# Up product of three of four feed-forward blocks as seven quarter products, with the conditioning pieces dealt out anew

## The chip, the cores and the metric

The kernel runs on one core of one Trainium2 chip. The metric is device time in microseconds (us) of one launch. TensorE (PE) does the matrix products, VectorE (DVE) and ScalarE (ACT) the elementwise work, GpSimd (POOL) small powers and some transfers, and SyncE's queue (SP) issues most of the weight loads. In the trace a weight load into TensorE is a row of PEld. Every float32 matrix instruction of 128 rows shows there as two entries, so that 32 instructions of the program are 64 entries of the trace.

## The reference

Two layers; in each, a feed-forward block, a token mixer, and a second feed-forward block. Touched are the feed-forward blocks and the conditioning:

```python
def swiglu(h, w13, w2):
    g, u = jnp.split(h @ w13, 2, axis=-1)
    return (jax.nn.silu(g) * u) @ w2
...
    for l in range(DEPTH):
        mod = (c_act @ ada_w[l] + ada_b[l]).reshape(bsz, N_SUB, 3, D_MODEL)
        h = modulated_norm(x, norm_w[l, 0], mod[:, 0])
        x = x + 0.5 * mod[:, 0, 2, None] * rmsnorm(swiglu(h, ffn_w13[l, 0], ffn_w2[l, 0]), norm_w[l, 1])
        h = modulated_norm(x, norm_w[l, 2], mod[:, 1])
...
        h = modulated_norm(x, norm_w[l, 4], mod[:, 2])
        x = x + 0.5 * mod[:, 2, 2, None] * rmsnorm(swiglu(h, ffn_w13[l, 1], ffn_w2[l, 1]), norm_w[l, 5])
```

There are 256 tokens, a width of 1024, an inner width of 2816; all is float32.

## The kernel before

A feed-forward block is named (l, f): layer l, first (f = 0) or second (f = 1) of the layer. It has an up phase and a down phase.

**Up phase.** The inner width is cut into FJ = 11 tiles j of 256 columns of gate and 256 columns of up. The weights of a tile (2 MB, two transfers) lie in one of two slots of `ring`. The normed input lies turned in `hT` (8 blocks of 128 channels, 256 tokens). Tile 0 is multiplied token half by token half as `hT` becomes ready (`open_by_token`, 64 products of 128 columns). The ten others go through `up(j)`: four outputs of 128 x 256, each a sum over 8 channel blocks, so 32 products of 256 moving columns. ScalarE takes the sigmoid of the gate half (its line 2037), VectorE makes sigmoid times gate times up in two operations into `actA` (line 2376). TensorE's tile j waits for the activation of tile j - 2, whose PSUM banks it takes over, and SP loads tile j + 2 when the product of tile j is done (line 735).

**Conditioning.** The modulation rows of later stages are vector-matrix products with 1024 x 1024 blocks of `ada_w`. Each row is streamed in four pieces of 1 MB (`PIECES`, three buffers, line 700), and VectorE multiplies and adds the two 128 x 1024 halves of a piece (`conditioning_pieces`, lines 2379 and 2382). When the four are done, TensorE sums over the partitions (`conditioning` in `beside`) and VectorE adds the bias. `COND_PLAN` says which rows belong to which block, `UP_PIECES` how many pieces follow each tile. All of them stood in the up phases.

**Down phase.** The product with `w2` is already made by seven quarter products of 512 moving columns (`down_1` to `down_7`), over six loads of weights (`DOWN_PAIRS`); VectorE makes sums of activations and of weights for each (`down_sums`, t and w). The last three keep two of the seven for the end (`HELD`). Then `after_down` forms the rows, the norm and the next stage's input.

The order of each engine is the order in which its code is written; there is no scheduler. VectorE's order in the up phase is the loop of `ffn` in its block: two operations of activation, evacuation of finished rows, pieces.

## Time and profile before

| | us |
|---|---|
| median of 3 runs | 2684.61 |
| lowest, highest | 2684.23, 2687.25 |
| the profiled execution | 2689.09 |
| span of its core in the profile | 2687.3 |
| TensorE busy | 2579.1 |
| VectorE busy | 1576.9 |

One execution is profiled. The span runs from its first to its last instruction; 1.8 us of the launch lie around it. A group row of the profile gives the number of entries, their busy time (overlapping ones counted once) and the mean duration of one. For pipelined matrix products the mean is longer than the distance from one to the next, so the pace of TensorE is read from the start of a run of equal entries and the start of the next run.

### The profile page before, as it was taken

What the parts mean: (1) busy time and instruction counts of PE and PEld (TensorE: products, weight loads), DVE (VectorE), ACT (ScalarE), POOL (GpSimd) and SP (SyncE); (2) the same over time, 40 slices, a digit from 0 to 9 for tenths busy, and PEclk for the clock granted to TensorE, in tenths of its full rate; (3) what the DMA queues carried; (4) which work ended last, traced back from release to release, by engine and by line L of the source; (5) the groups of instructions that cost most, each with busy time, mean ns of one, the idle gap of its engine ahead of it and who ended that gap; (6) DMA issues with size and microseconds to landing.
All of it is one profiled execution on the core that took longest, in us unless ns stands there. A gap on an engine that the chain in (4) does not pass through costs nothing.

```text
span 2687.3 us, 66122 instructions
## 1 busy us (share of the span) xinstructions
PE 2579.1 (96%) x29733; PEld 1889.3 (70%) x29733; DVE 1576.9 (59%) x2765; ACT 500.7 (19%) x1017; POOL 233.1 (9%) x372
## 2 busy tenths in 40 slices
PE   7999999999998999999999999999999999999998
PEld 6884877787775555588578758778778745556883
DVE  3566455677775866445644355556787758563225
ACT  1000232122221332100010011322222123321000
POOL 6000102000101101010000010110010011010000
PEclk9999999999899999999999999999999999999999
DMA  9885433222326543399576444423222275335443
GB/s 357 315 286 180 134 128 111 93 97 80 109 90 211 181 164 109 134 352 328 199 243 235 141 161 145 155 85 106 95 88 93 86 248 195 135 115 203 157 157 125
DMA packets 238987, 445.10 MB, mean 166 GB/s; under 512 B 8920, under 2 KB 103702, under 8 KB 238704
## 3 DMA queue, kind: packets, MB, share of 16 engines
...
## 4 chain that ended last, share of the span: by engine, by line
PE 82%; DVE 9%; DMA 3%; issue 3%; ACT 2%; SPq 1%; POOL 1%; DVEq 0%; POOLq 0%; ACTq 0%
PE ps L1152 80%; DVE scratch L2376 5%; DMA ring<-in_ffn_w 2%; DVE scratch L2379 1%; DVE scratch L2382 1%; DMA scratch<-acs_scratch 1%; DVE gbc L2382 1%; DMA ring<-in_w_in 1%; PE ps L1181 1%; DVE scratch L2728 1%; DMA acs_scratch<-scratch 0%; DVE x L2382 0%; PE ps L1834 0%; ACT scratch L2201 0%; ACT scratch L2199 0%
## 5 line engine op out<-in xcount | busy, mean ns | idle before, releaser
L1152 PE MATMUL ps<-hT,ring 64*64 64x256 f32 (+2 forms) x9216 | 1144.8, 373 | 9.9 <-issue 3.4
L1152 PEld LDWEIGHTS ps<-hT,ring 64*64 64x64 f32 (+1 forms) x9216 | 935.9, 159 | 147.6 <-issue 18.5
L1152 PE MATMUL ps<-scratch 64*64 64x32 f32 (+5 forms) x14824 | 661.7, 246 | 56.4 <-DVE scratch L2376 25.7
L1152 PEld LDWEIGHTS ps<-scratch 64*64 64x64 f32 (+2 forms) x14824 | 516.2, 140 | 240.9 <-issue 116.6
L1152 PE MATMUL ps<-ring,hT 64*64 64x256 f32 (+2 forms) x2816 | 425.4, 423 | 4.6 <-DVE scratch L2382 2.6
L2376 DVE TENSOR_TENSOR scratch<-scratch,ps 128x512 f32<-128x512 f32 (+2 forms) x324 | 163.0, 503 | 411.9 <-ACT scratch L2037 342.0
L1152 PE MATMUL ps<-ring,scratch 128*128 128x512 f32 x864 | 393.2, 594 | 2.8 <-DVE scratch L2379 1.3
L2376 DVE TENSOR_TENSOR scratch<-scratch 128x256 f32<-128x256 f32 (+4 forms) x522 | 314.7, 603 | 86.3 <-ACTq L2184 30.5
L1152 PEld LDWEIGHTS ps<-ring,hT 64*64 64x64 f32 (+1 forms) x2816 | 229.3, 151 | 141.2 <-issue 115.0
L1152 PEld LDWEIGHTS ps<-ring,scratch 128*128 128x128 f32 x864 | 158.8, 190 | 173.8 <-issue 165.9
L2382 DVE SCALAR_TENSOR_TENSOR scratch<-scratch,ccol 128x1024 f32<-128x1024 f32 x120 | 154.3, 1286 | 8.3 <-DMA scratch<-in_ada_w 4.1
L2037 ACT ACTIVATE scratch<-ps 128x512 f32<-128x512 f32 x44 | 26.3, 597 | 579.2 <-PE ps L1152 579.2
L2376 DVE TENSOR_TENSOR scratch<-ps,lvl 128x128 f32<-128x128 f32 (+1 forms) x224 | 73.8, 329 | 70.8 <-PE ps L1152 68.1
L2382 DVE SCALAR_TENSOR_TENSOR scratch<-ps,der,scratch 128x255 f32<-128x255 f32 (+1 forms) x112 | 54.0, 482 | 92.7 <-ACTq L2064 89.2
L2379 DVE TENSOR_SCALAR scratch<-scratch 128x64 f32<-128x64 f32 (+6 forms) x256 | 85.3, 333 | 38.1 <-ACTq L2350 14.4
L949 POOL TENSOR_TENSOR stat<-stat,mhalf 128x1 f32<-128x1 f32 x24 | 14.6, 609 | 931.8 <-DVE stat L2379 931.7
L2134 ACT ACTIVATE scratch<-ps 128x512 f32<-128x512 f32 x48 | 26.5, 595 | 256.8 <-PE ps L1152 256.8
L2376 DVE TENSOR_TENSOR scratch<-ring 128x1024 f32<-128x1024 f32 (+1 forms) x24 | 27.3, 1136 | 57.2 <-DMA ring<-in_ffn_w 57.0
L2062 ACT ACTIVATE scratch<-ps,der 128x256 f32<-128x256 f32 (+1 forms) x56 | 26.5, 473 | 146.6 <-PE ps L1152 145.3
L1042 POOL TENSOR_TENSOR scratch<-scratch 128x1024 f32<-128x1024 f32 x8 | 19.8, 2474 | 298.9 <-ACT scratch L2101 298.9
L2376 DVE TENSOR_TENSOR scratch<-ps,rmask 128x512 f32<-128x512 f32 x64 | 44.2, 691 | 2.2
L1027 POOL TENSOR_TENSOR scratch<-scratch,mhalf 128x4 f32<-128x4 f32 x16 | 16.6, 1037 | 309.5 <-DVE scratch L2379 309.5
...
## 6 DMA issues: line engine op xcount, KB each, us to landing
...
ring<-in_ffn_w SPq DMA_DIRECT2D x88, 1024.0 KB, 7.7
scratch<-in_ada_w SPq DMA_DIRECT2D x66, 1024.0 KB, 7.3
...
```

Source lines behind the costliest of these rows:

```text
L949: pool.tensor_tensor(stat[:, to + t:to + t + 1], stat[:, mean + t:mean + t + 1], mhalf[:, 0:1], ALU.pow).then_inc(rstd_ready.sem, 1)
L1027: pool.tensor_tensor(gstat[:, 3, :], gstat[:, 2, :], mhalf[:, 0:CH], ALU.pow).then_inc(gn_rstd.sem, 1)
L1042: pool.tensor_tensor(v, v, zsig, ALU.mult).then_inc(silu_product.sem, 1)
L1152: return pe.matmul(o, lhsT, rhs, start=start, stop=stop)
L1181: ins = pe.transpose(ps[:, 4 + 2 * t + kt // 4, (kt % 4) * P:(kt % 4 + 1) * P], of[:, t, kt * P:(kt + 1) * P], ident[:, :])
L2037: act.activation(sgm[:, j % 2, :], ps[:, 2 * ((j + 1) % 2), :], ACT.Sigmoid).then_inc(ffn_sig.sem, 1)
L2062: own.step(act.activation(dst, ps[0:cols, 2 * pair + m // 2, (m % 2) * S:(m % 2 + 1) * S], ACT.Identity, scale=der[0:cols, ds(mcol, 1)]))
L2134: act.activation(dst, ps[:, FILL_BANKS[r], :], ACT.Identity).then_inc(fill_evac.sem, 1)
L2376: return dve.tensor_tensor(o, i0, i1, op)
L2379: return dve.tensor_scalar(o, i0, s1, s2, op0, op1)
L2382: return dve.scalar_tensor_tensor(out=o, in0=i0, scalar=s, in1=i1, op0=op0, op1=op1)
L2728: own.step(dve.tensor_tensor_scan(gi.rearrange(f512), reset[:, :, :].rearrange("p a b -> p (a b)"), lwb.rearrange(f512), 0.0, ALU.mult, AL ...
```

## The change

In blocks (0, 1), (1, 0) and (1, 1) the tiles 1 to 10 go through `up_seven(j)`. The product is seen as 2 x 2 blocks: the channels in two halves, the columns as gate and up, the tokens in two halves. Seven products of quarters (m1 to m7, each 2 x 4 instructions of 128 moving columns) take the place of eight. Block (0, 0) and every tile 0 stay as they were.

VectorE makes four sums of the input once a block (`token_sums`) and four sums of weights per tile (`up_sums`), and puts the seven results together (`opening_sums`, `closing_sums`). The input's sums lie where the down phase keeps its own (`tsum`), the weights' sums where it keeps its sums of weights (`esets`), each tile in the set that the other parity's down sums use. ScalarE copies m1 out of PSUM (`first_up`) and takes the sigmoid of the finished sums of the tile before. In VectorE's order of iteration j stand: closing and gating of tile j - 1, the pieces, the opening of tile j, the weight sums of tile j + 1. The product m6 of tile j + 1 waits for those sums, m4 for ScalarE's copy and the input's sums. A ring slot is free after m7, with two of the seven products to go.

The pieces are 24, 24, 12 and 4 in the four blocks before, and 24, 16, 20 and 4 now, of which four each in (0, 1) and (1, 0) now follow the weight sums of the down phase. The last row of these two blocks is summed over the partitions in the down phase, before its last weights. In the first part of the down phase `down_5(0)` is behind `down_7(0)`.

```diff
 COND_PLAN = {(0, 0): tuple((0, k) for k in range(2, 8)),
-             (0, 1): ((0, 8),) + tuple((1, k) for k in range(5)),
-             (1, 0): tuple((1, k) for k in range(5, 8)),
+             (0, 1): ((0, 8), (1, 0), (1, 1), (1, 3)),
+             (1, 0): tuple((1, k) for k in (2, 4, 5, 6, 7)),
              (1, 1): ((1, 8),)}
 COND_ORDER = ((0, 0), (0, 1)) + tuple(itertools.chain(*(COND_PLAN[l, f] for l in range(DEPTH) for f in range(2))))
-UP_PIECES = (2, 2, 2, 3, 2, 3, 2, 3, 2, 3, 0)
+UP_PIECES = {(0, 0): (2, 2, 2, 3, 2, 3, 2, 3, 2, 3, 0),
+             (0, 1): (0, 1, 2, 1, 2, 1, 2, 1, 2, 0, 0),
+             (1, 0): (1, 2, 1, 2, 1, 2, 1, 2, 2, 2, 0),
+             (1, 1): (1, 1, 1, 1, 0, 0, 0, 0, 0, 0, 0)}
+DOWN_PIECES = {(0, 0): (0, 0, 0, 0, 0, 0), (0, 1): (0, 1, 2, 0, 1, 0), (1, 0): (0, 1, 2, 0, 1, 0), (1, 1): (0, 0, 0, 0, 0, 0)}
+SEVEN = {(0, 0): (), (0, 1): tuple(range(1, FJ)), (1, 0): tuple(range(1, FJ)), (1, 1): tuple(range(1, FJ))}
+SEVEN_ORDER = ("m1", "m2", "m4", "m6", "m7", "m5", "m3")
...
-                    pieces_next(UP_PIECES[j - 2])
+                    pieces_next(UP_PIECES[l, f][j - 2])
                 for i in range(DOWNS):
                     down_weights(i)
+                    pieces_next(UP_PIECES[l, f][FJ - 2 + i] if i < 2 else DOWN_PIECES[l, f][i - 2])
...
+                def up_seven(j):
+                    up_ready(j)
+                    par = ffn_item(f, j) % 2
+                    w = ring[:, par, :].rearrange("p (k u n) -> p k u n", k=KT, u=2)
+                    pair, third, sets = 2 * ((j + 1) % 2), 6 + j % 2, kset[j % 2]
+                    t0, t1, half = slice(0, P), slice(P, 2 * P), KT // 2
+                    def quarter(bank, side, weights, tokens):
+                        for m in range(2):
+                            at = 256 * side + m * P
+                            for k in range(half):
+                                ins = mm(ps[:, bank, at:at + P], weights(k, slice(m * P, m * P + P)), tokens(k), k == 0, k == half - 1)
+                        ins.then_inc(up_done.sem, 1)
+                    quarter(third, 0, lambda k, c: w[:, k, 0, c], lambda k: hT[:, k, t0])
+                    quarter(pair, 0, lambda k, c: w[:, half + k, 0, c], lambda k: hT[:, half + k, t0])
+                    pe.wait_ge(*copied(l, f, f"s1_{j}"))
+                    pe.wait_ge(*made(l, f, "turned"))
+                    quarter(third, 0, lambda k, c: w[:, half + k, 1, c], lambda k: turned_4[:, k, :])
+                    pe.wait_ge(*made(l, f, f"w_{j}"))
+                    quarter(pair, 1, lambda k, c: sets[1][:, k, c], lambda k: turned_2[:, k, :])
+                    quarter(pair + 1, 0, lambda k, c: w[:, k, 1, c], lambda k: turned_3[:, k, :])
+                    quarter(pair + 1, 1, lambda k, c: sets[0][:, k, c], lambda k: turned_1[:, k, :])
+                    quarter(third, 1, lambda k, c: sets[2][:, k, c], lambda k: hT[:, half + k, t1])
...
-                    up(j)
+                    if seven((l, f), j):
+                        up_seven(j)
+                    else:
+                        up(j)
...
-                early = [c for c in COND_PLAN[l, f] if c not in late_sums(l, f)]
+                early = [c for c in COND_PLAN[l, f] if c not in late_sums(l, f) + list(last_sums(l, f))]
                 pe.wait_ge(*cond_evac(0, cond_count(*early[-1])))
                 if f and l + 1 < DEPTH:
                     pe.wait_ge(*params_evac(l + 1, 1))
...
                 down_2(0)
                 pe.wait_ge(*down_sum(l, down_sum_count(f, "t0")))
                 sums_ready(0)
-                down_5(0)
+                pe.wait_ge(*made(l, f, f"act_{FJ - 2}"))
                 down_3(0)
-                pe.wait_ge(*act_ready(l, f * FJ + FJ - 1))
                 down_6(0)
                 down_7(0).then_inc(down_step.sem, 1)
-                pe.wait_ge(*act_ready(l, f * FJ + FJ))
+                pe.wait_ge(*made(l, f, f"act_{FJ - 1}"))
+                down_5(0)
                 down_4(0).then_inc(down_step.sem, 1)
                 for c in late_sums(l, f):
                     conditioning(*c, bank=2)
...
+                    if i == HELD[1]:
+                        for c in last_sums(l, f):
+                            conditioning(*c, bank=2)
...
+                def sigmoid_of_sums(j):
+                    act.wait_ge(*made(l, f, f"g_{j}"))
+                    act.activation(sgm[:, j % 2, :].rearrange("p (t n) -> p t n", t=TT), sums[:, j % 2, 0:4:3, :],
+                                   ACT.Sigmoid).then_inc(up_copied.sem, 1)
                 for j in range(FJ):
-                    if j >= 2:
-                        act.wait_ge(*act_ready(l, f * FJ + j - 1))
-                    act.wait_ge(*up_done(l, f * FJ + j + 1))
-                    act.activation(sgm[:, j % 2, :], ps[:, 2 * ((j + 1) % 2), :], ACT.Sigmoid).then_inc(ffn_sig.sem, 1)
+                    if seven((l, f), j):
+                        act.wait_ge(*product(l, f, f"m1_{j}"))
+                        act.activation(first_up[:, j % 2, :], ps[:, 6 + j % 2, 0:256], ACT.Identity).then_inc(up_copied.sem, 1)
+                        if seven((l, f), j - 1):
+                            sigmoid_of_sums(j - 1)
+                    else:
+                        if seven((l, f), j - 1):
+                            sigmoid_of_sums(j - 1)
+                        if j >= 2:
+                            act.wait_ge(*made(l, f, f"act_{j - 2}"))
+                        act.wait_ge(*product(l, f, f"up_{j}"))
+                        act.activation(sgm[:, j % 2, :], ps[:, 2 * ((j + 1) % 2), :], ACT.Sigmoid).then_inc(up_copied.sem, 1)
+                if seven((l, f), FJ - 1):
+                    sigmoid_of_sums(FJ - 1)
...
+                if i < 2 and seven((l, f), FJ - 1):
+                    dve.wait_ge(*product(l, f, f"m7_{FJ - 1}"))
...
+            def token_sums(l, f):
+                dve.wait_ge(*hT_act(l, hT_count(3 if f else 1, 1, KT // 2 - 1)))
+                b11, b12, b21, b22 = (hT[:, KT // 2 * i:KT // 2 * i + KT // 2, t * P:t * P + P] for i in range(2) for t in range(TT))
+                own.step(tt(turned_3, b22, b12, ALU.subtract))
+                own.step(tt(turned_1, b12, b11, ALU.subtract))
+                own.step(tt(turned_2, b22, turned_1, ALU.subtract))
+                raised(tt(turned_4, b21, turned_2, ALU.subtract), made(l, f, "turned"))
+            def up_sums(l, f, j):
+                item = ffn_item(f, j)
+                par = item % 2
+                w = ring[:, par, :].rearrange("p (k u n) -> p k u n", k=KT, u=2)
+                a11, a12, a21, a22 = (w[:, KT // 2 * i:KT // 2 * i + KT // 2, u, :] for u in range(2) for i in range(2))
+                s1, s2, s4 = kset[j % 2]
+                dve.wait_ge(*slot_loaded[par](l, loads_before(item, par) + 2))
+                own.step(tt(s1, a21, a22, ALU.add))
+                own.step(tt(a21, a11, a21, ALU.subtract))
+                own.step(tt(s2, s1, a11, ALU.subtract))
+                raised(tt(s4, a12, s2, ALU.subtract), made(l, f, f"w_{j}"))
             def ffn(l, f):
                 asked = conditioning_pieces(l, f)
+                def pieces_next(n):
+                    for _ in range(n):
+                        next(asked, None)
+                def side_by_side(bank):
+                    return ps[:, bank, :].rearrange("p (a n) -> p a n", a=2)
+                def opening_sums(j):
+                    dve.wait_ge(*copied(l, f, f"s1_{j}"))
+                    dve.wait_ge(*product(l, f, f"m6_{j}"))
+                    m1 = first_up[:, j % 2:j % 2 + 1, :].to_broadcast([P, 2, 256])
+                    own.step(tt(sums[:, j % 2, 0:4:2, :], m1, side_by_side(2 * ((j + 1) % 2)), ALU.add))
+                def closing_sums(j):
+                    pair, s = 2 * ((j + 1) % 2), sums[:, j % 2]
+                    dve.wait_ge(*product(l, f, f"m5_{j}"))
+                    own.step(tt(s[:, 1:4:2, :], s[:, 2:3, :].to_broadcast([P, 2, 256]), side_by_side(pair + 1), ALU.add))
+                    own.step(tt(s[:, 2, :], s[:, 1, :], ps[:, pair + 1, 256:512], ALU.add))
+                    dve.wait_ge(*product(l, f, f"m3_{j}"))
+                    raised(tt(s[:, 1:4:2, :], s[:, 1:4:2, :], side_by_side(6 + j % 2), ALU.add), made(l, f, f"g_{j}"))
+                def gated(j):
+                    by, s = sgm[:, j % 2, :].rearrange("p (t n) -> p t n", t=TT), sums[:, j % 2]
+                    dve.wait_ge(*copied(l, f, f"sig_{j}"))
+                    own.step(tt(by, by, s[:, 0:4:3, :], ALU.mult))
+                    for t in range(TT):
+                        ins = tt(actA[:, j, :, t * P:t * P + P], by[:, t, :].rearrange("p (m n) -> p m n", m=2),
+                                 s[:, 1 + t, :].rearrange("p (m n) -> p m n", m=2), ALU.mult)
+                        if t == 0:
+                            own.step(ins)
+                    raised(ins, made(l, f, f"act_{j}"))
+                    conditioned(j)
...
+                if SEVEN[l, f]:
+                    token_sums(l, f)
                 for j in range(FJ):
                     parity, bank = j % 2, 2 * ((j + 1) % 2)
+                    if seven((l, f), j - 1):
+                        closing_sums(j - 1)
+                        gated(j - 1)
+                    if seven((l, f), j):
+                        pieces_next(UP_PIECES[l, f][j])
+                        opening_sums(j)
+                    if seven((l, f), j + 1):
+                        up_sums(l, f, j + 1)
                     if j == FJ - 1:
                         down_sums(l, f, 0)
-                    dve.wait_ge(*ffn_sig(l, f * (FJ + 1) + j + 1))
-                    own.step(tt(sgm[:, parity, :], sgm[:, parity, :], ps[:, bank, :], ALU.mult))
-                    raised(tt(actA[:, j, :, :], sgm[:, parity, :], ps[:, bank + 1, :], ALU.mult), act_ready(l, f * FJ + j + 1))
-                    if f and l + 1 < DEPTH and j == 2:
-                        read_params(l + 1, 6)
-                        derive_params()
-                    for c in summed_in(l, f, j - 1) if j < FJ - 1 else ():
-                        conditioning(*c)
-                        if c == (l, 8):
-                            dve.wait_ge(*late_weights_loaded(l, 1))
-                            gate_weights(2, merged[:, 0, :])
-                        if c == (l + 1, 1):
-                            scale_weights(0)
-                    for _ in range(UP_PIECES[j]):
-                        next(asked, None)
+                    if not seven((l, f), j):
+                        dve.wait_ge(*copied(l, f, f"sig_{j}"))
+                        own.step(tt(sgm[:, parity, :], sgm[:, parity, :], ps[:, bank, :], ALU.mult))
+                        raised(tt(actA[:, j, :, :], sgm[:, parity, :], ps[:, bank + 1, :], ALU.mult), made(l, f, f"act_{j}"))
+                        conditioned(j)
+                        pieces_next(UP_PIECES[l, f][j])
+                if seven((l, f), FJ - 1):
+                    closing_sums(FJ - 1)
+                    gated(FJ - 1)
                 down_sums(l, f, 1)
                 for c in late_sums(l, f):
-                    conditioning(*c, bank=2)
+                    evacuate_conditioning(c, 2)
...
-                    scale_weights(1)
-                    scale_weights(2)
                     for i in range(2):
                         gate_weights(i, nbc[:, i, :])
+                pieces_next(DOWN_PIECES[l, f][1])
                 for i in range(2, DOWNS):
                     down_sums(l, f, i)
+                    pieces_next(DOWN_PIECES[l, f][i])
+                for c in last_sums(l, f):
+                    evacuate_conditioning(c, 2)
                 own.restart()
```

TensorE, the start of the up phase of block (0, 1): tile 0, then tiles 1 to 4 (`hT` input, `ring` weights, `scratch` sums, `prow` parameters, `ones` the sums over partitions). Before:

```order
L1152 MATMUL ps<-hT,ring 128x128 x36
L1152 MATMUL ps<-hT,ring 128x256 x64
L1212 MATMUL ps<-ident,prow 128x128 x4
L1152 MATMUL ps<-scratch,ones 128x512 x2
L1152 MATMUL ps<-hT,ring 128x256 x64
```

Now:

```order
L1230 MATMUL ps<-hT,ring 128x128 x52
L1230 MATMUL ps<-scratch,ring 128x128 x8
L1230 MATMUL ps<-scratch 128x128 x8
L1230 MATMUL ps<-scratch,ring 128x128 x8
L1230 MATMUL ps<-scratch 128x128 x8
L1230 MATMUL ps<-hT,scratch 128x128 x8
L1230 MATMUL ps<-hT,ring 128x128 x16
L1230 MATMUL ps<-scratch,ring 128x128 x8
```

Tile 1 is 56 instructions of 128 columns (the last 16 of the first row and the five rows of 8) where it was 32 of 256; m1 and m2 read what is loaded, the other five also sums that VectorE made.

VectorE in block (0, 1). Before, tiles 0 to 2: an activation in two operations, then the pieces:

```order
L2376 TENSOR_TENSOR scratch<-scratch,ps 128x512 x2
L2379 TENSOR_SCALAR scratch<-scratch,ccol 128x1024
L2382 SCALAR_TENSOR_TENSOR scratch<-scratch,ccol 128x1024 x3
L2376 TENSOR_TENSOR scratch<-scratch,ps 128x512 x2
L2382 SCALAR_TENSOR_TENSOR scratch<-scratch,ccol 128x1024 x4
L2376 TENSOR_TENSOR scratch<-scratch,ps 128x512 x2
```

Now, iteration 2: closing and gating of tile 1, two pieces, the opening of tile 2, the weight sums of tile 3:

```order
L2505 TENSOR_TENSOR scratch<-scratch,ps 128x2x256
L2505 TENSOR_TENSOR scratch<-scratch,ps 128x256
L2505 TENSOR_TENSOR scratch<-scratch,ps 128x2x256
L2505 TENSOR_TENSOR scratch<-scratch 128x512
L2505 TENSOR_TENSOR scratch<-scratch 128x2x128 x2
L2511 SCALAR_TENSOR_TENSOR scratch<-scratch,ccol 128x1024 x4
L2505 TENSOR_TENSOR scratch<-scratch,ps 128x2x256
L2505 TENSOR_TENSOR scratch<-ring 128x1024
L2505 TENSOR_TENSOR ring<-ring 128x4x256
L2505 TENSOR_TENSOR scratch<-scratch,ring 128x1024
L2505 TENSOR_TENSOR scratch<-ring,scratch 128x1024
```

Per tile VectorE has eleven operations besides the pieces, where it had two.

TensorE in the down phase of block (0, 1), from the first held weights to the last row's sum. Before:

```order
L1152 MATMUL ps<-ring,scratch 128x512 x8
L1152 MATMUL ps<-scratch 128x512 x2
L1152 MATMUL ps<-ring,scratch 128x512 x6
L1152 MATMUL ps<-scratch 128x512 x2
L1152 MATMUL ps<-ring,scratch 128x512 x4
```

Now:

```order
L1230 MATMUL ps<-ring,scratch 128x512 x8
L1230 MATMUL ps<-scratch 128x512 x2
L1230 MATMUL ps<-ring,scratch 128x512 x2
L1230 MATMUL ps<-ones,scratch 32x1 x32
L1230 MATMUL ps<-ring,scratch 128x512 x4
L1230 MATMUL ps<-scratch 128x512 x2
```

The sum of the last row stands between the second held weights and the last.

## Rows read from the trace of the kernel before

**Rows 1.** The page: busy time by engine, and the chain that ended last.
```profile
PE 2579.1 (96%) x29733; PEld 1889.3 (70%) x29733; DVE 1576.9 (59%) x2765; ACT 500.7 (19%) x1017; POOL 233.1 (9%) x372
PE 82%; DVE 9%; DMA 3%; issue 3%; ACT 2%; SPq 1%; POOL 1%; DVEq 0%; POOLq 0%; ACTq 0%
```

**Rows 2.** Stretches, tile 1 to the down phase: (0, 1), (1, 0), (1, 1). Header first.
```profile
core 0: us, PE busy (x) PEld busy (x) DVE busy (x) ACT busy (x) POOL busy (x), PEclk, DMA share, GB/s
1151.70:1296.30 144.60, 144.60 (x847) 125.36 (x847) 81.87 (x86) 5.97 (x10) 1.56 (x3) 1.00 0.89 317
1382.40:1524.00 141.60, 141.60 (x775) 123.68 (x775) 51.13 (x55) 5.97 (x10) 0.00 (x0) 1.00 0.63 216
2472.20:2612.10 139.90, 139.90 (x647) 122.55 (x647) 32.60 (x38) 5.97 (x10) 0.00 (x0) 1.00 0.49 161
```

**Rows 3.** Timeline of TensorE in block (0, 1): start, length, engine, line, entries.
```profile
1135.97 6.43 PE L1152 MATMUL ps<-hT,ring 128*128 128x128 f32 x56
...
1143.72 35.83 PE L1152 MATMUL ps<-hT,ring 128*128 128x128 f32 x200
...
1181.54 27.79 PE L1152 MATMUL ps<-hT,ring 128*128 128x256 f32 x128
1209.26 0.71 PE L1152 MATMUL ps<-ones,scratch 128*32 128x1 f32 x64
1209.90 27.89 PE L1152 MATMUL ps<-hT,ring 128*128 128x256 f32 x128
...
1252.29 1.88 PE L1152 MATMUL ps<-scratch,ones 128*128 128x512 f32 x4
1254.00 27.79 PE L1152 MATMUL ps<-hT,ring 128*128 128x256 f32 x128
```

**Rows 4.** First tile 0 of the program, TensorE by form; then its stretch's clock.
```profile
L1152 PE MATMUL ps<-hT,ring 128*128 128x128 f32 x128 | 17.0, 303 | 2.7 <-DMA ring<-in_ffn_w 2.7
...
34.60:52.00 17.40, 17.30 (x131) 17.25 (x132) 2.33 (x8) 1.58 (x5) 15.75 (x26) 0.85 1.04 395
```

**Rows 5.** VectorE by form, whole span: count, busy us, mean ns, idle before.
```profile
L2382 DVE SCALAR_TENSOR_TENSOR scratch<-scratch,ccol 128x1024 f32<-128x1024 f32 x120 | 154.3, 1286 | 8.3 <-DMA scratch<-in_ada_w 4.1
L2376 DVE TENSOR_TENSOR scratch<-scratch 128x512 f32<-128x512 f32 x188 | 134.1, 714 | 36.7 <-ACTq L2184 30.5
L2376 DVE TENSOR_TENSOR scratch<-scratch,ps 128x512 f32<-128x512 f32 x132 | 90.7, 687 | 359.7 <-ACT scratch L2037 342.0 <-PE ps L1152 15.0
L2376 DVE TENSOR_TENSOR scratch<-scratch 128x256 f32<-128x256 f32 x208 | 88.4, 425 | 23.9 <-PE ps L1152 14.3 <-POOL scratch L1027 2.4
L2376 DVE TENSOR_TENSOR scratch<-ring 128x1024 f32<-128x1024 f32 x20 | 24.5, 1225 | 51.8 <-DMA ring<-in_ffn_w 51.7
L2376 DVE TENSOR_TENSOR gbc<-gbc,ps 128x1024 f32<-128x1024 f32 x6 | 7.3, 1220 | 0.2
```

**Rows 6.** ScalarE by form, whole span: a copy out of PSUM, an activation in SBUF.
```profile
L2234 ACT ACTIVATE scratch<-ps 128x256 f32<-128x256 f32 x32 | 12.2, 382 | 109.3 <-PE ps L1152 109.3
L2212 ACT ACTIVATE scratch<-scratch 128x512 f32<-128x512 f32 x16 | 10.1, 630 | 64.0 <-DVE scratch L2376 64.0
```

**Rows 7.** Timeline of ScalarE and VectorE after tile 0 of block (0, 1).
```profile
1151.96 0.60 ACT L2037 ACTIVATE scratch<-ps 128x512 f32<-128x512 f32 x1 [5.23 <-PE ps L1152]
1152.59 1.41 DVE L2376 TENSOR_TENSOR scratch<-scratch,ps 128x512 f32<-128x512 f32 x2 [6.84 <-ACT scratch L2037]
1154.03 0.75 DVE L2379 TENSOR_SCALAR scratch<-scratch,ccol 128x1024 f32<-128x1024 f32 x1
```

**Rows 8.** The page: one of the transfers of a tile's weights, issue to landing.
```profile
ring<-in_ffn_w SPq DMA_DIRECT2D x88, 1024.0 KB, 7.7
```

**Rows 9.** The chain in order of time at the end of block (0, 1)'s down phase.
```profile
1337.38 6.57 DMA ring<-in_ffn_w
1344.04 1.24 DVE scratch L2376
...
1347.82 1.24 DVE scratch L2376
1349.19 13.97 PE ps L1152 x32
```

85 lines of the change are left out of this document (72 added, 13 removed).

## The prediction

> **What bounds the kernel now.** First the page's busy times and the chain that ended last: TensorE is busy for 96% of the span and makes up 82% of the chain, VectorE is busy for 59% [rows 1]. Then the three stretches that the change rewrites, from tile 1 to the down phase: TensorE is busy in every one of their 144.6, 141.6 and 139.9 us, and VectorE for 81.9, 51.1 and 32.6 us of them [rows 2]. So each microsecond taken from TensorE there is won, as long as VectorE and ScalarE keep pace, and VectorE has 63, 90 and 107 us to give. Third the timeline of TensorE: two tiles of 32 instructions start at 1181.54 and the next work at 1209.26, so a tile is 13.86 us and an entry of 256 columns 216.6 ns [rows 3].
>
> **TensorE's term.** A tile becomes 7 x 16 = 112 entries of 128 columns. The trace has such entries in tile 0: 56 in 6.43 us, of which the last 0.275 is its own drain, so 112 ns from one to the next; and in the run of 200 from 1143.72 the first 72 take 35.45 less 127 x 0.2166, or 7.94 us, 110 ns each [rows 3]. These runs have a wait every fourth instruction, so waits already met cost nothing visible. I take 111 ns: a quarter product is 1.78 us, a tile 12.43, a saving of 1.43 a tile and of 43 us for 30 tiles. That is the ceiling.
>
> The Trainium skill, "TensorE: Matmul & The Clock Gate", section "Back-to-back issue gap", speaks against products of so few columns: with a weight load each, 128 columns go at about 81 ns in bfloat16 where a lone product needs 56. By that ratio, an estimate from the page, an entry would be near 155 ns and a tile 17.4 us, 106 us lost in 30 tiles. The trace disagrees: half of 216.6 is 108.3, and 110 to 112 were measured with a fresh load before each [rows 3].
>
> **VectorE's term.** Per iteration it now has: closing 0.69 + 0.42 + 0.69; the sigmoid's way out and back 0.63 + 2 x 0.03, in which it waits; gating 0.71 + 2 x 0.425; opening 0.69; four weight sums of 1.225; with 0.03 between operations (1152.59 to 1154.03 for two of 0.69) [rows 5, 6, 7]. Sum: 1.89 + 0.69 + 1.65 + 0.72 + 5.02 = 9.97 us. A piece is two of 1.286, so 2.63, and 0.53 less for the first of a row, whose first half takes 0.75 [rows 5, 7]. A gate row's evacuation is 1.25, its scaling 1.3 [rows 5]. Against 12.43 us of TensorE: no piece fits with room, one makes 12.6, two make 15.2.
>
> The wait that decides is m6 of tile j + 1, 5.33 us into its tile, on the weight sums at the end of iteration j. Behind it stand m7, m5, m3 of the tile and all later tiles. I follow both engines with T the start of tile 1.
>
> Block (1, 1): iterations 4 to 10 have no piece. VectorE waits for m6 of its tile (T_j + 7.3), opens, makes the sums and is done 13.0 after T_j, 4.8 before they are wanted. The four single pieces end at 14.2 at worst, also in time. The up stretch is 10 x 12.43 + 1.72 for the gate row's sum (1254.00 less 1252.29) [rows 3] = 126.0, against 139.9. The down phase's first weight sums wait for m7 of tile 10, then take 6.8 us: ready 0.2 us late. **-13.6 us.**
>
> Block (0, 1): tile 2's weights are asked for at T, as the slot was tile 0's. I give them 8.5 us, the median 7.7 and the issue of two [rows 8]; so the sums of tile 2 are done at T + 13.5. Iterations 2 to 8: 7 x 9.97 = 69.8, eleven pieces less two firsts 27.9, parameter copy and rows 4.3: the sums of tile 9 are done at T + 115.5. TensorE alone would want them at 8 x 12.43 + 5.33 + 2.8 for transposes and rows = 107.5. So some 8 us of waits gather by tile 9, in pieces of 2 to 3; after it no tile has a piece and nothing is late. End: 115.7 + 7.1 + 12.43 + 0.7 = T + 135.9, first down wait 0.2, against 144.6. **-8.5 us.**
>
> Block (1, 0): its pieces begin in iterations 0 and 1 (1 and 2), so the sums of tile 2 end at T + 16.5. Iterations 2 to 9: 79.8, thirteen pieces less three firsts 32.6, rows 2.7: T + 131.6, where TensorE alone would want them at 9 x 12.43 + 5.33 + 4.1 = 121.3. Waits of 10.5 us, the largest about 4 before tile 10, whose two predecessors have two pieces each. End T + 138.9; the down phase's first sums come at 143.5 and are wanted at 142.3: + 1.2. Together 140.1 against 141.6; two small rows more in the down phase (0.64 each, 1209.90 less 1209.26 [rows 3]), one of which fills the wait before the last weights. **-0.6 us.** Here the whole gain of TensorE is given back.
>
> **Parts priced at nothing.** ScalarE's copy of m1 (0.38 [rows 6]) ends 2.4 us into a tile, m4 wants it at 3.6; cover 1.2. The input's four sums (2.9 us) and tile 1's weight sums (5.0) begin once `hT` is whole, some 2 us after 1143.72 [rows 3], and end 3 us before m6 of tile 1 wants them. The slot is freed two products before the end instead of at it, and the load has 11.6 us until VectorE wants it. SP's pieces wait for VectorE's sums, and are asked for three ahead; the weights queued behind them wait for a later m7 anyway. Eight pieces in two down phases, 21 us on VectorE: it enters the phase some 6 us later than before, and by my count is level by the second held weights. The phase ends in a chain over the last load: 6.6 us of transfer, 4.9 us of sums, then TensorE [rows 9]. VectorE must have its pieces behind it when that load lands; in (0, 1) by about 2 us, in (1, 0) by about 1. If not, each phase costs up to 2.6, one piece; bounds 0 and +5.
>
> Sum: -13.6 - 8.5 - 0.6 = -22.7; I take **-22**. The profiled span of 2687.3 becomes 2665, and the median, 2684.6, becomes **2662.6**; the profiled execution (2689.09) lay 4.5 above the median, and the difference is taken over.
>
> **Bounds of the unknown.** Entry: 110 to 133 ns, the latter from the first tile 0, 17.0 us for 128, but at a granted clock of 0.85 [rows 4]; I take 111, since all the stretches show 1.00 [rows 2]. Operations in 2 x 256 views of PSUM and on a broadcast stand in no row; nearest are 0.687 and 0.714 for plain 512 [rows 5]. Each 0.1 us more per iteration costs 0.9 in (0, 1) and 0.8 in (1, 0). Between -0.3 and +0.8 per iteration that is -5 to +14. Landing up to 12 us: +2. Each wait may bring a stretch at a lower clock: the first tile 0 lost 17.0 - 14.2 = 2.8 us so; for the two waits over 3 us at most +5.
>
> **The rivals.**
> 1. VectorE keeps up everywhere. For it: it is busy for only 59% now. Against: its iteration is a chain with two rounds to other engines. It needs 9.97 to shrink to near 9, as with a shorter sigmoid's way. Then 2684.6 - 41 = 2644.
> 2. Only (1, 1) gains. For it: eleven operations a tile behind semaphores, down phases with little room. At + 0.5 us per iteration and + 4 in the down phases: 2684.6 - 22 + 8.5 + 4 = 2675.
> 3. Slower: VectorE's iteration is the pace of (0, 1) and (1, 0), and above 11.3 us it gives back more than (1, 1) wins: 22 / 17 = 1.3 us more. At + 2 us, as if each of the three PSUM views and the split gating took half as long again and the engines' rounds 0.3 more, it is 2684.6 - 22 + 34 = 2697. Against: no row of VectorE shows a view that costs so much; the copies and sums of 512 all lie at 0.69 to 0.71 [rows 5].
> 4. The 128-column products pay for their weights after all: from 124 ns an entry, 13.86 a tile, nothing is won; at 133, +1.0 a tile, 2715. Against it stand the 184 entries of rows 3.
>
> **How the numbers follow.** Forecast (-14 to -32) 0.65; rival 1 (beyond -32) 0.07; rival 2 (-5.4 to -14) 0.13; no change within 5.4 us 0.08; rivals 3 and 4 0.07. 0.2% of the time, 5.4 us, is about what a measurement of this kernel tells from no change: faster 0.85, same 0.08, slower 0.07. The range takes the forecast with its bounds and rival 2: 2651 to 2679.
>
> **What would show it.** In the profile after: entries of 128 columns 110 to 112 ns apart; stretches of 136, 139 and 126 us; TensorE waiting for VectorE's weight sums (the operations `scratch<-ring,scratch`) 8 and 11 us in the first two and not at all in the third; waits at tiles 6, 7 and 9, and at 6, 8 and 10. VectorE idle before gating about 0.7 us a tile where it is late and 2 where it is not. The end of each down phase with a wait of at most 1.5 us. It would be wrong if an iteration without pieces is over 10.5 us, if tiles of (1, 1) are over 12.6, or if TensorE waits in the held part of a down phase.

## The result, and the profile after

The changed kernel takes 2671.59 us (median of four runs, 2668.59 to 2673.89) where the kernel before took 2684.65 beside it (four runs, 2684.23 to 2687.25). The ratio is 0.9949, with a 95% interval of 0.9931 to 0.9966: faster, by 13.1 us or half a per cent. Timed again, with five runs beside nine of before, it was 2670.49 against 2686.51, ratio 0.9941 (0.9924 to 0.9959), or 16.0 us. The forecast was 2662.6, a gain of 22, so 60 to 73% of the expected gain came, with a time inside the range.

The page of the profile after: busy times, and the shares of the chain that ended last.

```profile
PE 2544.8 (95%) x31173; PEld 1901.2 (71%) x31173; DVE 1812.4 (68%) x3047; ACT 513.3 (19%) x1047; POOL 235.2 (9%) x372
...
PE 72%; DVE 18%; DMA 4%; issue 3%; ACT 2%; SPq 1%; POOL 1%; DVEq 0%; POOLq 0%; ACTq 0%
```

Against [rows 1], TensorE has 34 us less to do, and the span fell by 21 (2687.3 to 2666.6). In the chain TensorE lost ten points, to VectorE above all: for part of the time VectorE now sets the pace. The three stretches of [rows 2], from tile 1 to the down phase, show where. Columns: the window and its length, busy time of PE, PEld, DVE, ACT and POOL, the granted clock, the DMA share and GB/s.

```profile
1145.90:1284.80 138.90, 131.80 (x1258) 129.62 (x1257) 121.11 (x144) 10.11 (x20) 1.52 (x3) 0.99 0.77 267
1371.00:1514.50 143.50, 135.05 (x1194) 132.05 (x1193) 129.42 (x146) 10.11 (x20) 0.00 (x0) 0.96 0.77 269
2464.80:2591.50 126.70, 126.70 (x1126) 125.74 (x1125) 99.67 (x120) 10.00 (x20) 0.00 (x0) 1.00 0.56 183
```

In (1, 1) TensorE is busy throughout and the stretch fell from 139.9 to 126.7. In (0, 1) it fell from 144.6 to 138.9, with 7.1 us of idle TensorE; in (1, 0) it grew from 141.6 to 143.5, with 8.4 us of idle TensorE and a granted clock of 0.96. VectorE is busy for 121 and 129 us there.

The timeline of TensorE in the up part of (1, 0), around tiles 6 and 10 (start, length, what; in brackets the idle time before and who ended it):

```profile
1444.43 2.81 PE L1230 MATMUL ps<-scratch 128*128 128x128 f32 x16 [2.19 <-DVE scratch L2505]
1447.03 2.86 PE L1230 MATMUL ps<-scratch,ring 128*128 128x128 f32 x16
...
1498.61 1.95 PE L1230 MATMUL ps<-scratch,ring 128*128 128x128 f32 x16
1504.54 3.78 PE L1230 MATMUL ps<-scratch 128*128 128x128 f32 x16 [3.98 <-DVE scratch L2505]
1508.11 3.03 PE L1230 MATMUL ps<-scratch,ring 128*128 128x128 f32 x16
1510.98 1.95 PE L1230 MATMUL ps<-scratch 128*128 128x128 f32 x16
1512.77 1.95 PE L1230 MATMUL ps<-hT,scratch 128*128 128x128 f32 x16
```

A quarter product at full clock is the last pair of rows: 1.79 us from one to the next, 111.7 ns an entry. Ahead of m6 TensorE waits for the weight sums, and in these two places the two quarters behind the wait take 6.4 us (1504.54 to 1510.98) and 5.3 (1444.43 to 1449.73) instead of 3.6. Such quarters are called slow below. The granted clock in the windows around the slow quarters of tiles 7 of (0, 1), 6 and 10 of (1, 0):

```profile
1233.50:1241.20 7.70, 5.50 (x35) 5.35 (x34) 6.69 (x9) 0.63 (x1) 0.00 (x0) 0.78 0.52 204
1442.00:1449.80 7.80, 5.61 (x36) 5.42 (x35) 6.79 (x9) 0.63 (x1) 0.00 (x0) 0.78 0.52 204
1500.40:1511.00 10.60, 6.62 (x35) 6.47 (x34) 8.00 (x11) 0.63 (x1) 0.00 (x0) 0.68 0.38 151
```

Cut into slices of 1 us, the trace has the granted clock at 0.50, the 1.2 GHz level, in part of each of them: from about 1237 to 1241, 1445.4 to 1449 and 1504.5 to 1510, behind waits of 2.19, 2.19 and 3.98 us.

To compare kernels I cut each trace at the start of the second part of tile 0 (the run that starts at 1143.72 in [rows 3]) and at the first down product. Up part and down part of each block, and the two mixers, whose code none of these kernels touches, in us:

| | (0, 1) | (1, 0) | (1, 1) | three blocks | two mixers |
|---|---|---|---|---|---|
| before | 152.6 + 78.1 | 149.6 + 77.3 | 147.9 + 75.2 | 680.7 | 1732.7 |
| before, again | 152.6 + 78.8 | 149.6 + 77.2 | 147.9 + 74.3 | 680.4 | 1727.0 |
| after | 147.0 + 78.2 | 151.6 + 79.0 | 134.8 + 75.1 | 665.6 | 1727.6 |
| after, again | 147.0 + 78.7 | 150.4 + 78.8 | 134.8 + 74.9 | 664.6 | 1726.3 |
| e1: (1, 1) only | 150.0 + 78.2 | 150.5 + 77.8 | 134.8 + 74.4 | 665.6 | 1736.7 |
| e2: not (1, 0) | 148.6 + 77.7 | 150.5 + 77.9 | 134.8 + 74.5 | 663.9 | 1729.2 |
| e3: half pieces | 137.0 + 77.4 | 137.4 + 78.2 | 134.8 + 75.0 | 639.8 | 1726.4 |
| e4: three whole tiles | 140.4 + 77.5 | 141.1 + 78.2 | 134.8 + 74.7 | 646.7 | 1726.3 |
| e4 again | 140.0 + 77.6 | 141.1 + 78.1 | 134.8 + 74.6 | 646.2 | 1729.5 |
| e5: m4 again | 146.9 + 77.4 | 148.8 + 79.8 | 134.8 + 75.1 | 662.8 | 1735.2 |
| e6: even deal, two whole | 137.8 + 78.9 | 138.7 + 82.4 | 134.8 + 74.5 | 647.2 | 1733.8 |
| e7: even deal | 139.1 + 83.1 | 146.5 + 83.4 | 134.8 + 75.3 | 662.2 | 1730.0 |
| e8: e6 and e4 joined | 137.8 + 80.1 | 140.7 + 79.5 | 134.8 + 75.1 | 648.0 | 1732.7 |

The mixers differ by up to 10 us between the profiles, and by 5.7 in two of the kernel before. So the 20.7 us between the first two profiled spans are not the change alone: the blocks, which repeat within about 1 us in two profiles of before, of after and of e4, give 680.5 less 665.1, or 15.4 us, between the two timed differences of 13.1 and 16.0. The mixers' length goes with the clock that they were granted: cut into eleven slices each, the second mixer has 1.00 in all of them in the second profile of after (861.5 us) and 0.96 to 0.98 in four in e1's (868.4), and the first mixer has 0.91 in one and 0.98 in three in the first profile of before (869.7) against 0.96 in one in the second (864.6), with the same code. From here on blocks are compared.

### The profile page after: what moved, and what is told of

It reads as the page before. It is cut to its first block, busy times and chain, and to the rows that moved or that the text cites. A ratio compares the mean times of both kernels' runs of the same rounds, so it can differ in the third digit from the quotient of the medians.

```text
span 2666.6 us, 69449 instructions
## 1 busy us (share of the span) xinstructions
PE 2544.8 (95%) x31173; PEld 1901.2 (71%) x31173; DVE 1812.4 (68%) x3047; ACT 513.3 (19%) x1047; POOL 235.2 (9%) x372
## 4 chain that ended last, share of the span: by engine, by line
PE 72%; DVE 18%; DMA 4%; issue 3%; ACT 2%; SPq 1%; POOL 1%; DVEq 0%; POOLq 0%; ACTq 0%
PE ps L1230 71%; DVE scratch L2505 10%; DVE scratch L2511 3%; DMA ring<-in_ffn_w 2%; DVE scratch L2508 1%; DVE ring L2505 1%; DVE gbc L2511 1%; DVE scratch L2943 1%; DMA ring<-in_w_in 1%; PE ps L1259 1%; DMA scratch<-acs_scratch 0%; DVE x L2511 0%; DMA acs_scratch<-scratch 0%; ACT scratch L2149 0%; ACT scratch L2330 0%
## 5 line engine op out<-in xcount | busy, mean ns | idle before, releaser
L1230 PE MATMUL ps<-hT,ring 64*64 64x256 f32 (+2 forms) x8256 | 839.3, 359 | 10.7 <-issue 4.6
L1230 PE MATMUL ps<-scratch 64*64 64x32 f32 (+8 forms) x15768 | 772.9, 246 | 70.4 <-DVE scratch L2505 37.0
L1230 PEld LDWEIGHTS ps<-scratch 64*64 64x64 f32 (+3 forms) x15768 | 622.9, 142 | 255.4 <-issue 116.4
L1230 PEld LDWEIGHTS ps<-hT,ring 64*64 64x64 f32 (+1 forms) x8256 | 680.8, 156 | 99.1 <-issue 19.5
L2505 DVE TENSOR_TENSOR scratch<-scratch 128x256 f32<-128x256 f32 (+5 forms) x612 | 361.1, 590 | 104.5 <-ACTq L2313 30.4
L1230 PEld LDWEIGHTS ps<-ring,hT 64*64 64x64 f32 (+1 forms) x2816 | 227.9, 150 | 139.9 <-issue 113.0
L2505 DVE TENSOR_TENSOR scratch<-scratch,ps 128x512 f32<-128x512 f32 (+2 forms) x384 | 196.3, 511 | 165.7 <-PE ps L1230 79.5
L1230 PE MATMUL ps<-scratch,ring 128*128 128x128 f32 x960 | 120.2, 280 | 0.0
L1230 PEld LDWEIGHTS ps<-scratch,ring 128*128 128x128 f32 x960 | 115.6, 197 | 0.0
L2505 DVE TENSOR_TENSOR scratch<-ring,scratch 128x1024 f32<-128x1024 f32 (+1 forms) x54 | 64.0, 1186 | 1.9
L2505 DVE TENSOR_TENSOR ring<-ring 128x1024 f32<-128x1024 f32 (+1 forms) x54 | 64.0, 1185 | 1.9
```

Source lines behind the costliest of these rows:

```text
L1230: return pe.matmul(o, lhsT, rhs, start=start, stop=stop)
L2505: return dve.tensor_tensor(o, i0, i1, op)
```

## The experiments

Theory at the start: VectorE's chain sets the pace of (0, 1) and (1, 0), so that seven products there give back on VectorE what they save on TensorE; only (1, 1) gains. Rivals: the waits come from weights or pieces that land late, or from the moved rows; and for the slow quarters, that the clock would fall without the waits.

**Where the gain sits.** Seven products in (1, 1) alone, the pieces dealt as in the changed kernel:

```diff
-SEVEN = {(0, 0): (), (0, 1): tuple(range(1, FJ)), (1, 0): tuple(range(1, FJ)), (1, 1): tuple(range(1, FJ))}
+SEVEN = {(0, 0): (), (0, 1): (), (1, 0): (), (1, 1): tuple(range(1, FJ))}
```

> Only block (1, 1) goes through seven quarter products; the pieces stay dealt out as in the changed kernel. Theory A (VectorE sets the pace of (0, 1) and (1, 0), and TensorE that of (1, 1)): the whole of -13.1 us of (1, 1) is kept, and the new deal of the pieces costs about nothing, so 2671 to 2673, no slower than the changed kernel. Rival B (TensorE's saving counts in all three blocks and the deal of the pieces or the down phases take it back): the time is 10 or more above that of the changed kernel, 2680 or more.

Measured: 2671.29 us, ratio 0.9947 (0.9929 to 0.9964), the changed kernel's time. Its three blocks take 665.6, as after. Rival B is out. The twenty tiles of (0, 1) and (1, 0) with one product less in eight bring next to nothing in sum: 2.8 us gained in (0, 1) (228.2 to 225.4, the mean of the two profiles of after), and 1.6 lost in (1, 0), a net 1.2 that is no more than two profiles of one kernel differ. The moved rows account for -2.8 and +1.4 there (against 231.0 and 226.8 before).

And (1, 0) alone left as whole products (`(1, 0): ()` in the same line):

> Seven quarter products in (0, 1) and (1, 1), whole products in (1, 0). Theory A: (1, 0) in quarters costs 143.5 us against 141.6 before, and 1.4 more at the start of its down phase; with whole products it takes about 143 by its two more rows: 1 to 3 us less than the changed kernel, 2668 to 2671. Rival B: (1, 0) is a part of the gain, and without it the time is 3 or more above the changed kernel's.

Measured: 2666.5 us, ratio 0.9926 (0.9907 to 0.9945), 4 to 5 us below the changed kernel where 1 to 3 were expected; the two intervals overlap, and the blocks show 1.2. So (1, 0) is no part of the gain.

**What makes the waits.** The second of the two multiply-adds of every piece is left out in (0, 1) and (1, 0), so half of each of those conditioning rows isn't summed; every load, wait and slot of the pieces stays:

```diff
-                    for m in range(each):
+                    for m in range(1 if (l, f) in ((0, 1), (1, 0)) else each):
```

> The changed kernel with the second multiply-add of each conditioning piece left out in the blocks (0, 1) and (1, 0), so VectorE has 1.3 us less a piece and the rows are wrong by half their terms; transfers, waits and TensorE's work stay. Theory A: TensorE's waits for the sums of weights, 7.1 and 8.5 us, go, and with them the stretches at a granted clock of 0.7 to 0.8; (0, 1) takes 129 us (from 138.9) and (1, 0) 129.5 (from 143.5), so 24 us less than the changed kernel, 2648. Rival C (the waits come from the loads of the weights or from SP's queue, which the pieces' transfers fill): the waits stay within 3 us of what they were and the time with them, 2668 or more.

Measured: 2644.84 us, ratio 0.9843 (0.9823 to 0.9863), where 2648 was expected. TensorE's busy time fills both stretches; the windows, columns as above:

```profile
1146.00:1275.00 129.00, 129.00 (x1259) 127.73 (x1258) 105.84 (x131) 9.88 (x20) 1.87 (x3) 1.00 0.84 288
1361.00:1490.00 129.00, 129.00 (x1191) 126.95 (x1191) 108.54 (x130) 9.80 (x20) 0.00 (x0) 1.00 0.85 299
```

In TensorE's timeline the only waits from tile 1 to the last products of the two blocks are these, at the end of the down phases:

```profile
1327.48 1.96 PE L1230 MATMUL ps<-scratch 128*128 128x512 f32 x4 [0.29 <-DVE scratch L2505]
...
1543.03 1.96 PE L1230 MATMUL ps<-scratch 128*128 128x512 f32 x4 [0.21 <-DVE scratch L2505]
```

The loads of weights and pieces are all still there, and no wait is left inside the up parts: VectorE's work is the cause. The up parts of 137.0 and 137.4 are TensorE's own price; the changed kernel lies 10.0 above it in (0, 1) and 13 to 14 in (1, 0).

**A version that gives VectorE time.** A tile as a whole product costs TensorE 1.35 us (13.86 less 12.51) and VectorE 8.6 less: an iteration of quarter products without pieces takes it 10.0 us, the two operations of a whole tile's activation 1.4. Tile 5 of (0, 1) and tiles 4 and 9 of (1, 0) are whole again:

```diff
+SEVEN = {(0, 0): (), (0, 1): (1, 2, 3, 4, 6, 7, 8, 9, 10), (1, 0): (1, 2, 3, 5, 6, 7, 8, 10), (1, 1): tuple(range(1, FJ))}
```

> The changed kernel with three tiles as whole products: tile 5 of (0, 1), tiles 4 and 9 of (1, 0). Theory A: a whole tile costs TensorE 1.35 us more and VectorE some 8 less, which is worth more where VectorE is late: (0, 1) from 138.9 to about 131, (1, 0) from 143.5 to about 133, so 15 to 18 us less than the changed kernel, 2654 to 2657. Rival B: 27 tiles save less than 30, so 4 us more than the changed kernel, 2676.

Measured: 2652.11 us, ratio 0.9876 (0.9854 to 0.9897); timed again 2651.19, ratio 0.9869 (0.9847 to 0.9892). That is better than expected (2654 to 2657). The up parts fall by 6.6 and 10.5 us, and no slow quarter is left. In place of waits of 15.5 us the up parts of the two blocks have these three, 2.4 us in all:

```profile
1189.24 2.05 PE L1230 MATMUL ps<-scratch 128*128 128x128 f32 x16 [1.35 <-DVE scratch L2505]
...
1256.17 2.05 PE L1230 MATMUL ps<-scratch 128*128 128x128 f32 x16 [0.27 <-DVE scratch L2505]
...
1460.04 2.05 PE L1230 MATMUL ps<-scratch 128*128 128x128 f32 x16 [0.82 <-DVE scratch L2505]
```

It is some 19 us faster than the changed kernel and 34 faster than before. Of the kernels here that compute the full result, only the last one below (e8) is as fast.

**The slow quarters.** The product m4 is computed once more ahead of m6 where TensorE would stand (tiles 6 and 7 of (0, 1), tile 6 of (1, 0)), and twice more at tile 10 of (1, 0):

```diff
+                    for _ in range({(0, 1, 6): 1, (0, 1, 7): 1, (1, 0, 6): 1, (1, 0, 10): 2}.get((l, f, j), 0)):
+                        for m in range(2):
+                            for k in range(half):
+                                mm(ps[:, third, m * P:m * P + P], w[:, half + k, 1, m * P:m * P + P], turned_4[:, k, :], k == 0, k == half - 1)
```

> Ahead of four of TensorE's waits for the opening sums, at tiles 6 and 7 of block (0,1) and at tiles 6 and 10 of block (1,0), the product m4 is computed once more into the same place (twice more at tile 10), with the same result: 16 more entries of 1.79 us, where TensorE otherwise stood for 2.5, 2.2, 2.2 and 4.0 us. Theory (a wait of over 2 us inside the tile is what lets the granted clock fall for the next quarter product): the added 9 us of work cost nothing, the waits shrink to 0.7, 0.4, 0.4 and 0.4, the slow quarters behind them are gone, and the kernel is 4 to 7 us faster than the changed kernel beside it, near 2665. Rival 1 (the clock falls for another reason, such as VectorE's load or the deal of the whole core): the slow quarters stay, and the time is that of the changed kernel within 1 us. Rival 2 (VectorE's sums come late because TensorE's early quarters are read or written against them in the same bank): more entries there put the sums later, and the time grows by 2 us or more.

Measured: 2673.28 us, ratio 0.9953 (0.9936 to 0.997), where the changed kernel beside it took 2670.49; the expected gain of 4 to 7 us isn't there. But behind the four filled gaps no slow quarter stands. Timeline and window of TensorE at tile 10 of (1, 0):

```profile
1500.29 5.52 PE L1230 MATMUL ps<-scratch,ring 128*128 128x128 f32 x48
1506.22 2.05 PE L1230 MATMUL ps<-scratch 128*128 128x128 f32 x16 [0.40 <-DVE scratch L2509]
1508.11 1.95 PE L1230 MATMUL ps<-scratch,ring 128*128 128x128 f32 x16
...
1500.30:1513.40 13.10, 12.70 (x114) 12.51 (x113) 11.68 (x17) 0.63 (x1) 0.00 (x0) 1.00 0.61 217
```

With TensorE busy, the granted clock stays at 1.00, in all four places; the 80 added entries, 8.9 us, cost the blocks nothing. This weighs most at tile 10 of (1, 0), where both profiles of the changed kernel have slow quarters. At the other three places one of those two profiles has none either (see below), and in this kernel's own profile the unfilled waits of 2.25 us at tile 9 of (0, 1) and 2.46 at tile 8 of (1, 0) have none. So for waits of that size one profile doesn't show what the filling did. Why it brings so little stands in VectorE's timeline at the same place, where the rows before the last are the weight sums of tile 10, first of the changed kernel:

```profile
1503.26 1.23 DVE L2505 TENSOR_TENSOR scratch<-ring,scratch 128x1024 f32<-128x1024 f32 x1
1504.52 1.86 DVE L2505 TENSOR_TENSOR scratch<-scratch,ps 128x512 f32<-128x512 f32 x3
```

and of this one:

```profile
1504.94 1.23 DVE L2509 TENSOR_TENSOR scratch<-ring,scratch 128x1024 f32<-128x1024 f32 x1
1506.20 1.86 DVE L2509 TENSOR_TENSOR scratch<-scratch,ps 128x512 f32<-128x512 f32 x3
```

Tile 1 starts at 1371.0 and 1372.7, so the sums end 133.5 us later in both. VectorE had not noticed the slow quarter of tile 6, since TensorE would have waited for it anyway. Only the slow quarters at tile 10, behind which no more waiting is left in the up part, reach its end: it is 148.8 against 151.6 and 150.4. In (0, 1) it is 146.9 against 147.0. The kernel e2, whose block (0, 1) has the changed kernel's code, shows the same without added work: in its profile slow quarters stand behind the last wait of that block, at tile 9, and its up part is 148.6 where the changed kernel's, without them there, is 147.0 both times:

```profile
1264.89 2.76 PE L1230 MATMUL ps<-scratch 128*128 128x128 f32 x16 [2.25 <-DVE scratch L2505]
1267.44 2.92 PE L1230 MATMUL ps<-scratch,ring 128*128 128x128 f32 x16
```

The 7 us by which this profile is longer than the changed kernel's second lie in the mixers (1735.2 against 1726.3), as in some kernels without this edit; whether the added work has a part in that is open.

The second profile of the changed kernel was to show whether the slow quarters belong to the waits:

> The changed kernel as it is, beside the next three runs. Its four runs so far gave 2668.6 to 2673.9. If the falls of the granted clock after the long waits (one of 1.7 us in block (0,1), 1.7 and 2.9 in block (1,0)) belong to the waits themselves, a second profiled execution shows them again behind tiles 7, 6 and 10. If they come from elsewhere (as the differences of several us between the mixers of the runs do), they sit at other tiles or are absent.

They came back, but not at all the same tiles: behind waits of 2.48 at tile 6 of (0, 1), 2.46 at tile 8 and 2.91 at tile 10 of (1, 0). Behind 2.25 at tile 9 of (0, 1) and 2.19 at tile 6 of (1, 0) there was none, though the same 2.19 had one in the first profile. So in these two profiles every slow quarter stands behind a wait of over 2 us, and not every such wait has one.

**The deal of the pieces.** One piece almost fits into a tile of 12.5 us, two don't. Spread as evenly as the sums allow, first with a whole product at tile 10 of (0, 1) and tile 5 of (1, 0):

```diff
-             (0, 1): (0, 1, 2, 1, 2, 1, 2, 1, 2, 0, 0),
-             (1, 0): (1, 2, 1, 2, 1, 2, 1, 2, 2, 2, 0),
+             (0, 1): (1, 1, 1, 1, 1, 1, 1, 1, 1, 2, 1),
+             (1, 0): (1, 2, 1, 2, 3, 2, 1, 1, 1, 1, 1),
```

> Only tables change. Conditioning pieces in block (0,1): 1 1 1 1 1 1 1 1 1 2 1 over tiles 0 to 10 instead of 0 1 2 1 2 1 2 1 2 0 0, and tile 10 is a whole product; in block (1,0): 1 2 1 2 3 2 1 1 1 1 1 instead of 1 2 1 2 1 2 1 2 2 2 0, and tile 5, where three pieces stand, is a whole product. By VectorE's recurrence (9.97 us an iteration and 2.63 a piece, 12.5 us a tile on TensorE) a tile with one piece is later by 0.1 us only, and what is late is taken back at the whole product. Theory: the wait at the down phase of block (0,1) comes at about 129.5 us after tile 0 (after: 137.8; three whole products: 130.2), that of (1,0) at about 132 (after: 143.3; three whole products: 132.1), with waits under 2 us everywhere, no slow quarters, and a time of 2648 to 2655, one whole product less for the same time as the version with three. Rival (a piece takes weights, a queue or a buffer at tiles 0, 9 and 10 that it didn't before, so that loads come late there): waits for DMA at tiles 9 to 11 and a time over 2658.

Measured: 2655.91 us, ratio 0.9888 (0.9869 to 0.9907), just above the expected 2648 to 2655. No wait inside the up parts is left, and they are 137.8 and 138.7, within 1.4 us of e3's. But in (1, 0) the down phase takes 4.2 us more than with e4's deal: TensorE waits 2.58 us there for VectorE's first weight sums and loses 1.7 more at a lowered clock. The rival, late loads at tiles 9 to 11, isn't seen: in both blocks TensorE waits for VectorE alone, and VectorE waits for a load in the up parts only at tile 2 of (0, 1), 1.36 us. Then with no whole product besides tile 0, and in (0, 1) the pieces 1 1 1 1 1 1 2 1 1 1 1:

> The even deal of the run before, with every tile but tile 0 by seven quarter products, as in the changed kernel. It tells whether the order of the pieces or the sum of VectorE's work sets the cost. Theory: in block (0,1) the sum nearly fits (12 pieces over 11 tiles) and the end comes at about 132 us (after: 137.8); in (1,0) 16 pieces over 11 tiles don't fit in any order, and the end stays at about 140 to 143. Time 2662 to 2667. Rival (the order of the pieces is of no account, only their number): the time of the changed kernel, 2669 to 2674.

Measured: 2671.95 us, ratio 0.9949 (0.9932 to 0.9966): the time of the changed kernel, as the rival has it, but not for its reason. In (0, 1) the up part is 7.9 us shorter, as the theory says (the down phase starts 131.0 after tile 1), and the down part 4.9 and 4.4 longer than in the two profiles of after. Timeline of TensorE at the start of that down phase:

```profile
1278.26 3.60 PE L1230 MATMUL ps<-ring,scratch 128*128 128x512 f32 x8
1285.08 1.47 PE L1230 MATMUL ps<-scratch 128*128 128x512 f32 x2 [3.22 <-DVE scratch L2505]
```

In VectorE's order a piece stands right before the sums of the first down weights (1274.60 to 1277.21), which end at 1284.98: TensorE waits 3.2 us and loses another 1.7 in the slow stretch behind it. A wait was moved past the point up to which I had reckoned. In (1, 0) the same happens: 5.1 and 3.9 us gained ahead against the two profiles of after, 4.4 and 4.6 given back. There the theory missed, since it had the up part unchanged; it falls although a wait of 6.1 us stands at tile 5, behind the three pieces. The three blocks together gain 3 us.

Last the better block of each version, with e6's line for (0, 1), e4's for (1, 0):

> The better block of two versions put together: block (0,1) with the even deal and only tile 10 as a whole product (its block took 216.8 us, against 217.9 with the deal of the changed kernel and tile 5 whole), block (1,0) with the changed kernel's deal and tiles 4 and 9 whole (219.3, against 221.1 with the even deal, which left a wait of 2.6 us at the down phase and 2.2 us of lowered clock behind it). If the blocks are independent, the sum of the blocks is 1.1 us below the version with three whole products, so about 2651, not to be told from it. If the difference between 2652.1 and 2655.9 of those two versions came from block (0,1), it is near 2656.

Measured: 2650.11 us, ratio 0.9869 (0.9848 to 0.989), beside 2651.19 for the version with three whole tiles: not to be told apart, and in the blocks 1.3 to 1.8 more rather than 1.1 less. With the same tables (0, 1) took 1.1 us more than in e6 and (1, 0) 0.9 more than in e4, as much as two profiles of one kernel differ, so the two deals of (0, 1) can't be ranked.

## Why the prediction was right, and where it was not

**TensorE's term: right.** Entries 111.7 ns apart against 111 taken, so a tile 12.51 instead of 12.43, 0.8 us more in each block. The Trainium skill, "TensorE: Matmul & The Clock Gate", section "Back-to-back issue gap", speaks for a penalty for the weights of such short products; these traces show 3%, with two entries of 128 columns costing 223 ns where one of 256 costs 216.6.

**(1, 1): right.** Forecast -13.6, measured -12.9 by the means of two profiles each (209.8 against 222.7); the 0.8 of the tiles is the difference. No wait inside, as foreseen.

**(0, 1): right in mechanism, mis-sized.** Forecast -8.5, measured -5.6. The stretch is 138.9 against my 135.9. The term that was mis-sized is VectorE's recurrence: the sums of tile 9 were to be done at T + 115.5, and are at T + 118.3 (T = 1145.9). VectorE's timeline around tile 2 and at the last tile without pieces:

```profile
1156.05 1.23 DVE L2505 TENSOR_TENSOR scratch<-ring 128x1024 f32<-128x1024 f32 x1 [2.04 <-DMA ring<-in_ffn_w]
1157.31 1.23 DVE L2505 TENSOR_TENSOR ring<-ring 128x1024 f32<-128x1024 f32 x1
1158.57 1.22 DVE L2505 TENSOR_TENSOR scratch<-scratch,ring 128x1024 f32<-128x1024 f32 x1
1159.83 1.22 DVE L2505 TENSOR_TENSOR scratch<-ring,scratch 128x1024 f32<-128x1024 f32 x1
...
1264.20 1.86 DVE L2505 TENSOR_TENSOR scratch<-scratch,ps 128x512 f32<-128x512 f32 x3
1266.83 1.61 DVE L2505 TENSOR_TENSOR scratch<-scratch 128x512 f32<-128x512 f32 x3 [0.77 <-ACT scratch L2149]
1268.48 0.69 DVE L2505 TENSOR_TENSOR scratch<-scratch,ps 128x512 f32<-128x512 f32 x1
1269.20 1.22 DVE L2505 TENSOR_TENSOR scratch<-ring 128x1024 f32<-128x1024 f32 x1
1270.46 1.22 DVE L2505 TENSOR_TENSOR ring<-ring 128x1024 f32<-128x1024 f32 x1
1271.72 1.22 DVE L2505 TENSOR_TENSOR scratch<-scratch,ring 128x1024 f32<-128x1024 f32 x1
1272.97 1.22 DVE L2505 TENSOR_TENSOR scratch<-ring,scratch 128x1024 f32<-128x1024 f32 x1
1274.23 1.86 DVE L2505 TENSOR_TENSOR scratch<-scratch,ps 128x512 f32<-128x512 f32 x3
```

Tile 2's weights are there at T + 10.15, not 8.5: 1.7 us. The iteration is 10.03 (1264.20 to 1274.23), not 9.97: 0.4 in seven. Three waits of 0.21 at pieces, for which I had no term: 0.6. Sum 2.7, all of it on the path, because from T + 15 on VectorE never catches up. The first two were within the bounds I gave, and were not taken into the value.

**(1, 0): the sign was wrong.** Forecast -0.6, measured +3.7 and +2.4 against the mean of before. The sums of tile 10 were to be done at T + 131.6 and are at T + 133.5 (T = 1371.0), 1.9 us later: 0.4 already at tile 2, 0.5 by eight longer iterations, 0.8 by four waits at pieces. The other step that failed is the granted clock. I had bounded it at +5 for two waits and counted it as nothing in the sum. What it costs is 1.6 to 2.8 us (the up part of 150.4 and 151.6 against 148.8 with m4 repeated), behind the wait at tile 10. The wait for the first down weight sums, put at 1.2, was 0 with the slow quarters and 1.07 without them: they had taken its place. The down part grew by 1.6: the two rows take 1.5 there, and of the wait at its end, which one of them was to fill, only 0.3 to 0.5 went. The rest, 0.5 to 0.6 us, is not accounted for.

**Slips in the working.** The 128-column entries in [rows 3] are 128 (56 and 72), not 184. In (1, 0), 140.1 against 141.6 and one row of 0.64 is -0.9, not -0.6. And 0.1 us more per iteration is 0.7 us in (0, 1), by the seven iterations counted there, not 0.9, so that the bounds of that term are -4.5 and +12. None changes the reading.

**Signs.** Waits of 8 and 11 us: 7.1 and 8.4, and with them 1.7 and 4.6 of slow quarters. At tiles 6, 7 and 9, and 6, 8 and 10: yes, with smaller ones at 4 and 5, and at 5 and 9. VectorE idle before gating 0.77 where it is late: yes. Waits at the end of the down phases under 1.5: 1.04, 0.94 and 1.25 in the first profile, 1.57, 0.75 and 1.08 in the second, so one is just over. Pieces in the down phases for nothing: in (0, 1) the down part is as before (78.2 and 78.7 against 78.1 and 78.8); in (1, 0) the 1.6 above leave room for some 0.6.

**The rivals.** The second, that only (1, 1) gains, describes the result better than the forecast does: -12.9 of -15.4 lie there, and e1 has the same time. Its time, 2675, was nearer to 2671.6 than 2662.6 is, and the first timed gain, 13.1, lies in the band that I had given to it (5.4 to 14), the second, 16.0, in that of the forecast. I had reached it by VectorE's operations being dearer, and gave it 0.13; what made it nearly true was smaller things that all fell on the same side, because a chain that is late has no slack to take them, and the lowered clock behind the last wait. That the forecast's range held in spite of a wrong sign in (1, 0) owes to (1, 1), which was right, and to the width of the range. The first rival (2644) would have needed VectorE to keep up, which it did with half of each piece left out (2644.84).
